# Row scaling folded into TensorE's turning of the token tiles, with a new loading and issue order at the start of a hybrid stream encoder

## The chip, the cores and the metric

The kernel runs on one core of one Trainium2 chip. The metric is the device time of that core in microseconds (us). A core has five engines with instruction streams of their own: TensorE (PE, matrix products, with its weight loads shown as PEld), VectorE (DVE), ScalarE (ACT), GpSimd (POOL) and SyncE (SP, which here only issues DMAs). They wait for each other through semaphores.

## The reference: one encoder step over 1024 + 64 tokens

The input is 1024 prompt rows and 64 sample rows of 2048 float32 numbers. Every row is first scaled to unit root mean square and by a vector, then multiplied by a wide matrix:

```python
def rmsnorm(x, g):
    r = lax.rsqrt(jnp.mean(xf * xf, axis=-1, keepdims=True) + EPS)
    return (xf * r * g.astype(jnp.float32)).astype(x.dtype)

h = rmsnorm(x, norm_g)
proj = jnp.einsum('btd,dc->btc', h, w_in)          # 2048 -> 10240 columns
xa, za, v, bg, cg, zb, ga, gb = jnp.split(proj, SPLIT_IDX, axis=-1)
ya = pool_mixer(xa) * silu(za)                     # trailing means over 2/4/8/16 frames, then a map
yb = bg * conv3(cg * v) * silu(zb)
merged = sigmoid(ga) * (ya @ w_proj_pool) + sigmoid(gb) * (yb @ w_proj_conv)
x = x + merged @ w_out
y = rmsnorm(x, final_norm_g)
```

Only the first `rmsnorm` and the first few products with `w_in` are touched by the change.

## The kernel before, in words

**Products.** All matrix products run in a rounded float32 type (f32r). To keep float32 accuracy each operand is held as a high part and a low part (what the high part leaves over), and each product is three terms: high weights by high tokens, high weights by low tokens, low weights by high tokens (`terms`, line 1323). One such product is 24 matmuls of 128 x 272. The big product is further divided by a recursive scheme that saves block products, so sums and differences of operand blocks are made on DVE. Weights come by DMA into three `raw` tiles, ACT makes the high part (`split_hi`, line 1573), DVE the low part (`split_lo`, line 1983), and DVE forms sums of weight blocks in three `sb` tiles (`weight_sum`).

**The opening.** The 1088 tokens are nine tiles `xn[0]` to `xn[8]` of 128 rows (the last has 64); in the listings of instructions they are called xn_104 to xn_112. Each tile goes through five steps:
1. two DMA queues (SP's and ACT's) load it, 1 MB a tile;
2. ACT squares it and sums each row (`square`, line 1870);
3. POOL makes `var` and `rstd`, one number a row (lines 1168 and 1171);
4. DVE or ACT multiplies the whole tile by `rstd` (`scale`, lines 2548 and 1877), in place;
5. TensorE turns it, 128 x 128 at a time (`turn`, line 1488): the tile's block is the stationary operand and the identity moves, in TensorE's transposing form. One turn (t, a) is eight such blocks, the half a of the columns of tile t, written to one of two PSUM tiles; `copy_turned` (lines 2560 and 2562, one on ACT at 1886) multiplies by `norm_g` on the way to SBUF.

There are 18 turns, two a tile. Their order stands in a table, `TURNS`, which PE and DVE both follow; turn i waits until turn i-2 has been copied out. Of the turns 11 stand ahead of the first product and the other seven between the first products. `turn_vectors` (lines 1494 and 1497) turns the small vectors and the state rows. Once the halves a = 0 of the tiles 0 to 4 are copied, `first_operand_hi(0)` (ACT, line 1648) and `first_operand_lo(0)` (DVE, line 2143) make the first token operand, and the first product can start. The first two weight groups use eight products each, from four operands f = 0 to 3; operand f = 2 needs the halves a = 0 of all nine tiles. From there on the kernel is a long list of products in a fixed order.

**Who sets the order.** No scheduler: each engine's instructions stand in the order of the code, and the waits are written by hand. The two queues and the lists of calls on ACT and DVE at the start are what the change rewrites.

Of the kernel before, what the change touches and what calls it, by code (L numbers as in the profile page):

```python
# [10 lines left out]
P = 128  # L11
# [4 lines left out]
def bass_hybrid_stream_step(nc, x_prompt, x_sample, state_pool, state_conv, norm_g, w_in, b_gate,  # L16
# [156 lines left out]
    for m in range(2 * NP):  # L173
        RAW_TILE[m] = (m if m < 3 else RAW_TILE[RAW_BEFORE[m]] if m in RAW_BEFORE else
                       RAW_Y if m == COUPLE_H1 else RAW_X)
        RAW_COUNT[m] = 1 + sum(RAW_TILE[k] == RAW_TILE[m] for k in range(m))
# [49 lines left out]
    with ExitStack() as ctx:  # L226
# [83 lines left out]
        sb = at("sb", SB0, [3, KQ * P])  # L310

# [140 lines left out]
        x_scaled_act = sem("x_scaled_act")  # L452
        x_scaled_dve = sem("x_scaled_dve")
# [120 lines left out]
        def prep_source(n):  # L574
# [10 lines left out]
            if q in (0, 5, 6):  # L585
# [262 lines left out]
        def _(sp):  # L848
# [294 lines left out]
        def _(pool):  # L1143
# [21 lines left out]
            for t in SQUARE_TURN:  # L1165
# [6 lines left out]
                    .then_inc(rstd_made, 1)  # L1172

# [136 lines left out]
        def _(pe):  # L1310
# [166 lines left out]
            def turn(i):  # L1477
# [50 lines left out]
            for i in range(11):  # L1528
                if i == 4:
# [3 lines left out]
            i = 11  # L1533
            for g in range(NC):
                for k, turns in enumerate((0, 0, 2, 4, 1, 0, 0, 0) if g == 0 else (0,) * 8):
# [25 lines left out]
        def _(act):  # L1561
# [298 lines left out]
            for t in (0, 1):  # L1860
                act.dma_start(xn[t][:, D // 2:D], x_rows(t)[:, D // 2:D]).then_inc(x_landed[t], 16)
# [824 lines left out]
```

## Time and profile before

| | |
|---|---|
| median of 3 runs | 2418.03 us (2417.90 to 2418.84) |
| the profiled execution | 2418.74 us |
| its span | 2416.9 us |
| PE busy | 99% of the span |
| DVE, ACT, POOL busy | 70%, 37%, 5% |
| mean granted TensorE clock | 0.997 of full |
| HBM read, written | 281.00 MB, 133.77 MB |

The profile is one execution. Times in it count from the start of the span. "Busy" of an engine excludes waiting and DMA issuing. A row of a timeline gives the start, the time from its first instruction's start to its last one's end, the line, the operation, the tile written and the tiles read, the count, and in brackets how long the engine had been idle and what released it. The duration of a single matmul record contains its latency, which neighbours overlap; what a matmul costs in a stream is read from the starts of two successive groups.

### The profile page before, as it was taken

To read this page: it belongs to the slowest core of one execution; us is meant where nothing else is said; L and a number is where in the kernel's file an instruction comes from. 1 tells how busy PE (TensorE), PEld (TensorE's weight loads), DVE (VectorE), ACT (ScalarE), POOL (GpSimd) and SP (SyncE) were. 2 spreads that over 40 slices of the span, in tenths; PEclk is the share of its full clock that TensorE was granted. 3 is DMA by queue.
4 is the path that set the end of the run, shared out by engine and by line. 5 is a ranking of instruction groups with operands and counts; after the bars stand their busy time and mean duration, and the time that the engine had idled before them with its cause. 6 is when DMAs were issued, how large, how long until landed. Compare 5 with 4: busy or idle time off the path is not lost.

```text
span 2416.9 us, 42656 instructions
## 1 busy us (share of the span) xinstructions
PE 2392.0 (99%) x17810; PEld 2331.3 (96%) x17810; DVE 1701.1 (70%) x2330; ACT 894.1 (37%) x1308; POOL 114.5 (5%) x218
## 2 busy tenths in 40 slices
PE   7999999999999999999999999999999999999998
PEld 7999999999999999999999999999999999888886
DVE  6676666666666686777868777765755887887676
ACT  6433333333333343323322222233533533532535
POOL 2010000000000000000000000000000011100000
PEclk9999999999999999999999999999999999999999
DMA  6663323232323454434433333245655768898656
GB/s 220 234 216 104 113 97 120 90 127 90 125 92 116 165 197 144 157 136 146 155 132 113 136 133 139 100 161 208 223 169 168 276 242 282 295 344 304 245 179 226
DMA packets 195695, 418.05 MB, mean 173 GB/s; under 512 B 12489, under 2 KB 113917, under 8 KB 180656
## 3 DMA queue, kind: packets, MB, share of 16 engines
q1 hardware_dynamic: 170672, 284.85, 35.1%
q0 software_dynamic: 23744, 125.24, 13.7%
q10 hardware_dynamic: 1088, 5.24, 0.6%
q8 instruction: 142, 2.33, 0.4%
q14 instruction: 49, 0.40, 0.1%
HBM read 281.00 MB, written 133.77 MB: 172 GB/s over the span
## 4 chain that ended last, share of the span: by engine, by line
PE 98%; DMA 1%; DVE 1%; issue 0%; ACT 0%; POOL 0%; ACTq 0%; DVEq 0%; POOLq 0%
PE ps L1323 76%; PE ps L1450 12%; PE ps L1365 7%; PE ps L1472 1%; PE ps L1512 1%; DMA xn<-in_x_prompt_dram 1%; PE ps L1488 0%; DVE ops L2143 0%; ACT ops L1648 0%; ACT junk L1870 0%; DVE out L2406 0%; DVE h0raw L2560 0%; DVE out L2459 0%; DVE xn L2548 0%; POOL rstd L1304 0%
## 5 line engine op out<-in xcount | busy, mean ns | idle before, releaser
L1323 PE MATMUL ps<-ops,hi 128*128 128x272 f32 x9760 | 1329.8, 288 | 0.2 <-DVE ops L2143 0.2
L1323 PEld LDWEIGHTS ps<-ops,hi 128*128 128x128 f32 x9760 | 1268.7, 188 | 0.7 <-DVE ops L2143 0.7
L1323 PE MATMUL ps<-ops,lo 128*128 128x272 f32 x4880 | 710.9, 288 | 0.0
L1323 PEld LDWEIGHTS ps<-ops,lo 128*128 128x128 f32 x4880 | 649.6, 188 | 0.0
L1573 ACT ACTIVATE hi<-sb 128x512 fp32r<-128x512 f32 x440 | 278.2, 632 | 579.0 <-PE ps L1323 444.2
L2123 DVE TENSOR_TENSOR pb<-pb,ps 128x544 f32<-128x544 f32 x330 | 237.4, 720 | 261.5 <-PE ps L1323 261.4
L1983 DVE TENSOR_TENSOR lo<-sb,hi 128x512 fp32r<-128x512 f32 x440 | 303.1, 689 | 151.4 <-ACT hi L1573 146.7
L1573 ACT ACTIVATE hi<-raw 128x512 fp32r<-128x512 f32 x264 | 166.7, 632 | 371.2 <-PE ps L1323 357.2
L1983 DVE TENSOR_TENSOR lo<-raw,hi 128x512 fp32r<-128x512 f32 x264 | 181.7, 689 | 104.4 <-ACT hi L1573 104.4
L1450 PE MATMUL ps<-ms_hi,mt 128*128 128x512 f32 x896 | 221.3, 389 | 0.0
L1450 PEld LDWEIGHTS ps<-ms_hi,mt 128*128 128x128 f32 x896 | 168.1, 188 | 34.9
L2041 DVE TENSOR_TENSOR pb<-pb,ps 128x544 f32<-128x544 f32 (+1 forms) x176 | 108.2, 614 | 69.7 <-PE ps L1323 66.2
L1590 ACT COPY pb<-ps 128x544 f32<-128x544 f32 (+1 forms) x160 | 83.6, 523 | 152.3 <-PE ps L1323 134.6
L2019 DVE TENSOR_TENSOR sb<-raw 128x512 f32<-128x512 f32 x183 | 125.3, 685 | 5.1 <-DMA raw<-in_w_in_dram 5.1
L1450 PE MATMUL ps<-ms_lo,mt 128*128 128x512 f32 x448 | 119.7, 389 | 0.0
L1619 ACT COPY pb<-ps 128x544 f32<-128x544 f32 x88 | 53.9, 612 | 157.1 <-PE ps L1323 141.2
L2406 DVE TENSOR_TENSOR out<-out,ps 128x512 f32<-128x512 f32 x100 | 68.1, 682 | 59.2 <-PE ps L1450 59.2
L1734 ACT CAST ms_hi<-ms 128x2048 fp32r<-128x2048 f32 x32 | 61.2, 1911 | 108.0 <-DVE ms L2354 73.4
L1450 PEld LDWEIGHTS ps<-ms_lo,mt 128*128 128x128 f32 x448 | 84.1, 188 | 17.5
L1365 PE MATMUL ps<-ops,hi 128*128 128x272 f32 x512 | 74.6, 288 | 0.0
L1740 ACT CAST mt<-mt_raw 128x2048 fp32r<-128x2048 f32 x28 | 53.5, 1910 | 54.0 <-DMA mt_raw<-opq 32.4
L2364 DVE TENSOR_TENSOR ms_lo<-ms,ms_hi 128x2048 fp32r<-128x2048 f32 x32 | 73.1, 2284 | 0.0
(164 smaller groups left out, 1564.6 us busy)
## 6 DMA issues: line engine op xcount, KB each, us to landing
raw<-in_w_in_dram SPq DMA_DIRECT2D x157, 512.0 KB, 3.9
pb<-part SPq DMA_DIRECT2D x39, 1088.0 KB, 6.8
part<-pb POOLq DMA_DIRECT2D x37, 1088.0 KB, 5.2
mt_raw<-opq SPq DMA_DIRECT2D x28, 1024.0 KB, 6.2
gates<-pb POOLq DMA_DIRECT2D x16, 1088.0 KB, 9.2
gate<-gates SPq DMA_DIRECT2D x32, 544.0 KB, 6.2
ms<-in_w_out_dram SPq DMA_DIRECT2D x16, 1024.0 KB, 9.9
ops_raw<-opq SPq DMA_DIRECT2D x15, 1088.0 KB, 7.3
```

What stands on the lines that cost most here:

```text
L1323: mm = nc.tensor.matmul(ps[b][:, c, 0:HC], w[:, w_slot, kt * P:(kt + 1) * P], operand[:, kt, half, c * HC:(c + 1) * HC], start=fresh and k ...
L1365: mm = nc.tensor.matmul(ps[b][:, c, 0:HC], w[:, s % R, k * P:(k + 1) * P], operand[:, kt, half, :], start=i in (0, 1, 5) and kt == 0 and w ...
L1450: mm = nc.tensor.matmul(dst, mt[n % 3][:, kt, half, t * P:(t + 1) * P], own[:, kt, :], start=fresh and kt == 0 and w is ms_hi and half == ...
L1573: nc.scalar.activation(split_of(hi, n), src, ACT.Copy).then_inc(w_hi, 1)
L1590: nc.scalar.copy(dst, src).then_inc(act_drained, 1)
L1734: nc.scalar.copy(ms_hi[(USES * p + e) % 3][:, :, :], src[:, :, :]).then_inc(ms_hi_made, 1)
L1983: nc.vector.tensor_tensor(split_of(lo, n), src, f32(split_of(hi, n)), ALU.subtract).then_inc(w_lo, 1)
L2019: nc.vector.tensor_tensor(sb_of(g, q), a, b, op).then_inc(s_made, 1)
L2041: each = nc.vector.tensor_tensor(own, own, src, ALU.add)
L2123: nc.vector.tensor_tensor(target(s), target(s), psum(s), ALU.add).then_inc(dve_drained, 1)
L2364: nc.vector.tensor_tensor(ms_lo[held][:, :, :], source_of(p, e)[:, :, :], f32(ms_hi[(USES * p + e) % 3][:, :, :]), ALU.subtract).then_inc( ...
L2406: nc.vector.tensor_tensor(own, own, m_tile(p, q, t), ALU.add).then_inc(m_added, 1)
```

## The change

The scaling of step 4 goes. Instead POOL multiplies the identity by `rstd` into a 128 x 128 tile `diag[t]`, and the turn multiplies by that in place of the identity. The turn is then no longer issued in the transposing form but as an ordinary float32 matmul: its result is the turned block with each token's column scaled. The nine diagonals lie where the `sb` tiles lie, so the first weight sum waits until all turns are done, and the fourth waits for `w_lo`.

All tiles are loaded in two column halves, the first half by SP and the second by ACT, in the order of the tiles; the first weight tile is loaded in two halves too, after tile 4 (`EARLY` is 5). ACT issues its halves of tiles 5 to 8 after its first two squares. The tables and the lists of calls are rewritten.

```diff
@@ at line 308 @@
+        diag = [at(f"diag{t}", SB0 + t * P * 4, [P]) for t in range(TT)]
@@ the order of the turns, of the squares @@
-        TURNS = ((0, 0), (0, 1), (1, 1), (1, 0), (3, 0), (2, 0), (4, 0), (2, 1), (3, 1),
-                 (5, 0), (5, 1), (7, 1), (7, 0), (8, 0), (8, 1), (6, 0), (4, 1), (6, 1))
+        TURNS = ((0, 1), (1, 1), (1, 0), (2, 0), (2, 1), (3, 0), (0, 0), (4, 0), (3, 1),
+                 (4, 1), (5, 0), (5, 1), (7, 0), (7, 1), (6, 0), (8, 0), (6, 1), (8, 1))
-        SQUARE_TURN = (0, 1, 3, 2, 4, 5, 7, 8, 6)
+        SQUARE_TURN = (0, 1, 2, 3, 4, 5, 7, 6, 8)
-        SCALED_ACT = (1, 5, 8, 6)
-        SCALED_DVE = (0, 3, 2, 4, 7)
-        COPIED_ACT = ((4, 1),)
+        COPIED_ACT = ((8, 1),)
@@ SP @@
-            for t in (0, 1):
-                sp.dma_start(xn[t][:, 0:D // 2], x_rows(t)[:, 0:D // 2]).then_inc(x_landed[t], 16)
-            for t in (3, 5):
-                sp.dma_start(xn[t][:, :], x_rows(t)).then_inc(x_landed[t], 16)
-            load_weights(0)
-            sp.dma_start(xn[7][:, :], x_rows(7)).then_inc(x_landed[7], 16)
+            for t in range(TT):
+                if t == EARLY:
+                    sp.dma_start(raw_pair(0)[:, 0:2, :], weights_of(0, 0)[:, 0:2, :]).then_inc(raw_landed[RAW_TILE[0]], 16)
+                sp.dma_start(xn[t][0:rows(t), 0:D // 2], x_rows(t)[:, 0:D // 2]).then_inc(x_landed[t], 16)
@@ POOL @@
+                pool.wait_ge(rstd_made, SQUARED_AT[t])
+                nc.gpsimd.tensor_scalar(diag[t][0:r, 0:r], ident[0:r, 0:r], rstd[0:r, t:t + 1], None, ALU.mult) \
+                    .then_inc(diag_made, 1)
@@ PE @@
-                if t in SCALED_ACT:
-                    pe.wait_ge(x_scaled_act, SCALED_ACT.index(t) + 1)
-                else:
-                    pe.wait_ge(x_scaled_dve, SCALED_DVE.index(t) + 1)
+                pe.wait_ge(diag_made, SQUARED_AT[t])
                 if i >= 2:
                     wait_copied(pe, i - 1)
                 for k in range(KE):
-                    mm = nc.tensor.transpose(flat[2 + i % 2][:, k * P:k * P + r],
-                                             xn[t][0:r, (a * KE + k) * P:(a * KE + k + 1) * P], ident[0:r, 0:r])
+                    mm = nc.tensor.matmul(flat[2 + i % 2][:, k * P:k * P + r],
+                                          xn[t][0:r, (a * KE + k) * P:(a * KE + k + 1) * P], diag[t][0:r, 0:r],
+                                          start=True, stop=True)
@@ PE, the turns ahead of and between the first products @@
-            for i in range(11):
-                if i == 4:
+            for i in range(12):
+                if i == 1:
                     turn_vectors()
-                for k, turns in enumerate((0, 0, 2, 4, 1, 0, 0, 0) if g == 0 else (0,) * 8):
+                for k, turns in enumerate((0, 2, 2, 1, 1, 0, 0, 0) if g == 0 else (0,) * 8):
@@ ACT @@
-            for t in (0, 1):
-                act.dma_start(xn[t][:, D // 2:D], x_rows(t)[:, D // 2:D]).then_inc(x_landed[t], 16)
-            for t in range(2, TT, 2):
-                act.dma_start(xn[t][0:rows(t), :], x_rows(t)).then_inc(x_landed[t], 16)
+            def load_second_half(t):
+                act.dma_start(xn[t][0:rows(t), D // 2:D], x_rows(t)[:, D // 2:D]).then_inc(x_landed[t], 16)
+
+            for t in range(EARLY):
+                load_second_half(t)
+            act.dma_start(raw_pair(0)[:, 2:4, :], weights_of(0, 0)[:, 2:4, :]).then_inc(raw_landed[RAW_TILE[0]], 16)
-            def scale(t):
-                r = rows(t)
-                own = xn[t][0:r, :]
-                act.wait_ge(rstd_made, SQUARED_AT[t])
-                nc.scalar.activation(own, own, ACT.Copy, scale=rstd[0:r, t:t + 1]).then_inc(x_scaled_act, 1)
@@ DVE @@
+                if SUM_COUNT[g, q] == 1:
+                    dve.wait_ge(x_turned, len(TURNS))
+                if SUM_COUNT[g, q] == 4:
+                    dve.wait_ge(w_lo, split_of_slot(NC * NQ + 1))
-            def scale(t):
-                r = rows(t)
-                own = xn[t][0:r, :]
-                dve.wait_ge(rstd_made, SQUARED_AT[t])
-                nc.vector.tensor_scalar(own, own, rstd[0:r, t:t + 1], None, ALU.mult).then_inc(x_scaled_dve, 1)
...
```

What it moves is seen in the engines' instruction lists. First PE, from the first turn on, before (xn_104 is tile 0, xn_105 tile 1; each pair of rows is one turn of eight blocks):

```order
L1488 MATMUL ps<-ident,xn_104 128x128 [waits x_scaled_dve]
L1488 MATMUL ps<-ident,xn_104 128x128 x7
L1488 MATMUL ps<-ident,xn_104 128x128 [waits x_scaled_dve]
L1488 MATMUL ps<-ident,xn_104 128x128 x7
L1488 MATMUL ps<-ident,xn_105 128x128 [waits h_copied_dve,x_scaled_act]
L1488 MATMUL ps<-ident,xn_105 128x128 x7
L1488 MATMUL ps<-ident,xn_105 128x128 [waits h_copied_dve,x_scaled_act]
L1488 MATMUL ps<-ident,xn_105 128x128 x7
L1494 MATMUL ps<-ident,vec_rows 128x64 [waits rows_landed]
L1497 MATMUL ps<-ident,state_rows 128x17 x8
```

and the same place now (diag_127 to diag_135 are the nine diagonals):

```order
L1484 MATMUL ps<-diag_127,xn_104 128x128 [waits diag_made]
L1484 MATMUL ps<-diag_127,xn_104 128x128 x7
L1491 MATMUL ps<-ident,vec_rows 128x64 [waits rows_landed]
L1494 MATMUL ps<-ident,state_rows 128x17 x8
L1484 MATMUL ps<-diag_128,xn_105 128x128 [waits diag_made]
L1484 MATMUL ps<-diag_128,xn_105 128x128 x7
L1484 MATMUL ps<-diag_128,xn_105 128x128 [waits h_copied_dve,diag_made]
L1484 MATMUL ps<-diag_128,xn_105 128x128 x7
L1484 MATMUL ps<-diag_129,xn_106 128x128 [waits h_copied_dve,diag_made]
L1484 MATMUL ps<-diag_129,xn_106 128x128 x7
```

The small turns of the vectors and the state, which wait for GpSimd's small loads, stand behind one turn now and stood behind four; tile 0's other half has gone to the seventh place.

Next PE behind the first product, before (its last term, the second product, and the turn of tile 7, which is xn_111):

```order
L1323 MATMUL ps<-ops,lo 128x272 [waits w_lo]
L1323 MATMUL ps<-ops,lo 128x272 x7
L1323 MATMUL ps<-ops,hi 128x272 [waits first_hi,w_hi,setup_copied]
L1323 MATMUL ps<-ops,hi 128x272 x7
L1323 MATMUL ps<-ops,hi 128x272 [waits first_lo]
L1323 MATMUL ps<-ops,hi 128x272 x7
L1323 MATMUL ps<-ops,lo 128x272 [waits w_lo]
L1323 MATMUL ps<-ops,lo 128x272 x7
L1488 MATMUL ps<-ident,xn_111 128x128 [waits h_copied_dve,x_scaled_dve]
L1488 MATMUL ps<-ident,xn_111 128x128 x7
```

and now:

```order
L1322 MATMUL ps<-ops,lo 128x272 [waits w_lo]
L1322 MATMUL ps<-ops,lo 128x272 x7
L1484 MATMUL ps<-diag_134,xn_111 128x128 [waits h_copied_dve,diag_made]
L1484 MATMUL ps<-diag_134,xn_111 128x128 x7
L1484 MATMUL ps<-diag_134,xn_111 128x128 [waits h_copied_dve,diag_made]
L1484 MATMUL ps<-diag_134,xn_111 128x128 x7
L1322 MATMUL ps<-ops,hi 128x272 [waits first_hi,w_hi,setup_copied]
L1322 MATMUL ps<-ops,hi 128x272 x7
L1322 MATMUL ps<-ops,hi 128x272 [waits first_lo]
L1322 MATMUL ps<-ops,hi 128x272 x7
```

Two turns now stand between the first and the second product; the six that are left after the first product come one or two at a time.

Last DVE's start, before:

```order
L2548 TENSOR_SCALAR xn_104<-xn_104,rstd 128x2048 [waits rstd_made]
L2567 COPY g_col<-ps 128x16 [waits g_turned]
L2560 TENSOR_TENSOR h0raw<-ps,g_col 128x8x128 [waits g_made,x_turned]
L2562 TENSOR_TENSOR h1raw<-ps,g_col 128x2x4x128 [waits g_made,x_turned] x2
L2560 TENSOR_TENSOR h0raw<-ps,g_col 128x8x128 [waits g_made,x_turned]
L2573 COPY state<-ps 128x136 [waits setup_turned]
L2548 TENSOR_SCALAR xn_107<-xn_107,rstd 128x2048 [waits rstd_made]
L2548 TENSOR_SCALAR xn_106<-xn_106,rstd 128x2048 [waits rstd_made]
L2560 TENSOR_TENSOR h0raw<-ps,g_col 128x8x128 [waits g_made,x_turned]
```

and now:

```order
L2557 COPY g_col<-ps 128x16 [waits g_turned]
L2559 COPY state<-ps 128x136 [waits setup_turned]
L2553 TENSOR_TENSOR h1raw<-ps,g_col 128x2x4x128 [waits g_made,x_turned] x2
L2564 COPY vec<-ps 128x64 [waits setup_turned]
L2551 TENSOR_TENSOR h0raw<-ps,g_col 128x8x128 [waits g_made,x_turned] x2
L2553 TENSOR_TENSOR h1raw<-ps,g_col 128x2x4x128 [waits g_made,x_turned]
L2551 TENSOR_TENSOR h0raw<-ps,g_col 128x8x128 [waits g_made,x_turned] x3
```

DVE has no scaling left, only copies; the copy of the state rows, which was behind four copies of turns, is ahead of all of them.

## Rows read from the trace of the kernel before

**Rows 1.** The page, engine totals: busy us, share of the span, instructions.

```profile
PE 2392.0 (99%) x17810; PEld 2331.3 (96%) x17810; DVE 1701.1 (70%) x2330; ACT 894.1 (37%) x1308; POOL 114.5 (5%) x218
```

**Rows 2.** Stretches: length, busy us by engine, clock, DMA share, GB/s.

```profile
8.19:30.86 22.67, 16.79 (x99) 14.61 (x99) 17.01 (x16) 17.84 (x16) 4.72 (x11) 0.85 1.03 360
30.86:50.75 19.89, 19.28 (x164) 18.58 (x162) 16.90 (x16) 15.33 (x14) 3.75 (x6) 1.00 0.19 59
50.75:87.00 36.25, 36.25 (x288) 36.25 (x289) 25.31 (x18) 18.01 (x26) 3.67 (x5) 1.00 0.51 184
```

**Rows 3.** The chain of waits, 0 to 75 us: start, us, what.

```profile
2.15 17.32 DMA xn<-in_x_prompt_dram
...
22.44 1.30 DVE xn L2548
...
37.58 1.75 PE ps L1488 x16
```

**Rows 4.** Timeline of ACT, the opening.

```profile
5.82 1.91 ACT L1870 ACTIVATE junk<-xn 128x2048 f32<-128x2048 f32 x1 [0.35 <-DMA xn<-in_x_prompt_dram]
...
8.91 1.91 ACT L1870 ACTIVATE junk<-xn 128x2048 f32<-128x2048 f32 x1 [1.09 <-DMA xn<-in_x_prompt_dram]
...
19.49 1.91 ACT L1870 ACTIVATE junk<-xn 128x2048 f32<-128x2048 f32 x1 [1.25 <-DMA xn<-in_x_prompt_dram]
...
27.05 2.01 ACT L1648 CAST ops<-h0raw 128x2176 fp32r<-128x2176 f32 x1 [0.51 <-DVE h0raw L2560]
```

**Rows 5.** Timeline of GpSimd (POOL), the opening.

```profile
1.18 0.29 POOL L1146 TENSOR_SCALAR_AFFINE_SELECT ident<-ident 128x128 f32<-128x128 f32 x1 [0.25 <-POOL ident L1144]
...
5.34 0.50 POOL L1163 DMA_DIRECT2D state_rows<-in_state_conv_dram  x1
7.91 0.18 POOL L1168 TENSOR_SCALAR var<-ssq 128x1 f32<-128x1 f32 x1 [2.07 <-ACT junk L1870]
8.18 0.56 POOL L1171 TENSOR_TENSOR rstd<-var,power 128x1 f32<-128x1 f32 x1
```

**Rows 6.** DMA issues, 0 to 75 us: count, KB each, us to landing.

```profile
state_rows<-in_state_conv_dram POOLq DMA_DIRECT2D x1, 8.0 KB, 9.4
```

**Rows 7.** Timeline of PE: turns and products.

```profile
10.12 6.15 PE L1488 MATMUL ps<-ident,xn 128*128 128x128 f32 x32 [1.67 <-DVE xn L2548]
16.20 0.27 PE L1494 MATMUL ps<-ident,vec_rows 64*128 64x64 f32 x1
16.40 0.66 PE L1497 MATMUL ps<-ident,state_rows 17*128 17x17 f32 x8
...
21.01 1.92 PE L1488 MATMUL ps<-ident,xn 128*128 128x128 f32 x8 [0.91 <-DVE xn L2548]
...
42.27 1.22 PE L1488 MATMUL ps<-ident,xn 64*128 64x64 f32 x16
...
73.99 2.18 PE L1323 MATMUL ps<-ops,hi 128*128 128x272 f32 x16
76.01 1.17 PE L1323 MATMUL ps<-ops,lo 128*128 128x272 f32 x8
77.01 2.18 PE L1323 MATMUL ps<-ops,hi 128*128 128x272 f32 x16
```

**Rows 8.** Timeline of PE, the last phase, 128x512 products.

```profile
2150.80 1.98 PE L1450 MATMUL ps<-ms_hi,mt 128*128 128x512 f32 x8
2152.61 1.07 PE L1450 MATMUL ps<-ms_lo,mt 128*128 128x512 f32 x4
2153.52 1.98 PE L1450 MATMUL ps<-ms_hi,mt 128*128 128x512 f32 x8
```

**Rows 9.** Timeline of DVE, the opening.

```profile
8.78 1.29 DVE L2548 TENSOR_SCALAR xn<-xn,rstd 128x2048 f32<-128x2048 f32 x1 [8.78 <-POOL rstd L1171]
...
12.12 1.23 DVE L2560 TENSOR_TENSOR h0raw<-ps,g_col 128x1024 f32<-128x1024 f32 x1 [1.98 <-PE ps L1488]
...
29.80 2.42 DVE L2143 TENSOR_TENSOR ops<-h0raw,ops 128x2176 fp32r<-128x2176 f32 x1
```

**Rows 10.** Stretches of two us, columns as in rows 2.

```profile
20.00:22.00 2.00, 1.09 (x6) 0.99 (x6) 2.00 (x2) 1.91 (x3) 0.33 (x2) 0.78 1.14 386
22.00:24.00 2.00, 1.15 (x6) 0.75 (x5) 1.65 (x3) 1.59 (x2) 0.64 (x3) 0.50 0.99 204
...
26.00:28.00 2.00, 2.00 (x11) 1.93 (x10) 1.52 (x2) 1.49 (x2) 0.00 (x0) 0.52 0.99 411
```

More of the change, by code:

```diff
@@ L175, in bass_hybrid_stream_step @@
                        RAW_Y if m == COUPLE_H1 else RAW_X)
-        RAW_COUNT[m] = 1 + sum(RAW_TILE[k] == RAW_TILE[m] for k in range(m))
+        RAW_COUNT[m] = 1 + sum(RAW_TILE[k] == RAW_TILE[m] for k in range(m)) + (RAW_TILE[m] == RAW_TILE[0])
     def operands_of(ph, o):
@@ L1891, in _ @@
             square(0)
+            load_second_half(5)
+            load_second_half(6)
             square(1)
-            scale(1)
+            load_second_half(7)
+            load_second_half(8)
+            square(2)
             square(3)
-            square(2)
             square(4)
             square(5)
-            scale(5)
+            split_hi(SLOT0)
             first_operand_hi(0)
-            split_hi(SLOT0)
             split_hi(SLOT0 + 1)
             square(7)
+            square(6)
+            split_hi(SLOT0 + 2)
+            square(8)
+            split_hi(SLOT0 + 3)
             first_operand_hi(1)
-            square(8)
-            split_hi(SLOT0 + 2)
-            square(6)
-            scale(8)
-            scale(6)
-            split_hi(SLOT0 + 3)
+            first_operand_hi(2)
             drain(SLOT0)
-            first_operand_hi(2)
             first_operand_hi(3)
             drain(SLOT0 + 1)
-            copy_turned(4)
+            split_hi(SLOT0 + 4)
+            copy_turned(8)
             drain(SLOT0 + 2)
-            split_hi(SLOT0 + 4)
             split_hi(SLOT0 + 5)
+            split_hi(SLOT0 + 6)
+            split_hi(SLOT0 + 7)
+            drain(SLOT0 + 3)
             first_operand_hi(4)
-            split_hi(SLOT0 + 6)
-            drain(SLOT0 + 3)
-            split_hi(SLOT0 + 7)
-            first_operand_hi(5)
             drain(SLOT0 + 4)
             drain(SLOT0 + 5)
+            first_operand_hi(5)
+            first_operand_hi(6)
             split_hi(NC * NQ)
-            first_operand_hi(6)
+            drain(SLOT0 + 6)
             split_hi(NC * NQ + 1)
+            first_operand_hi(7)
             split_hi(NC * NQ + 2)
-            drain(SLOT0 + 6)
-            first_operand_hi(7)
             for s in range(NC * NQ, NS):
@@ L2574, in _ @@
                 "p (j n) -> p j n", n=32)[:, :, 0:HALO]).then_inc(setup_copied, 1)
-            scale(3)
-            scale(2)
+            copy_turned(TURNS.index((0, 1)))
+            copy_turned(TURNS.index((1, 1)))
+            dve.wait_ge(setup_turned, 2)
+            nc.vector.tensor_copy(vec[:, :], flat[1][:, 0:NVEC]).then_inc(setup_copied, 1)
+            copy_turned(TURNS.index((1, 0)))
+            copy_turned(TURNS.index((2, 0)))
+            copy_turned(TURNS.index((2, 1)))
             copy_turned(TURNS.index((3, 0)))
-            scale(4)
@@ L2588, in _ @@
+            copy_turned(TURNS.index((7, 0)))
             split_lo(SLOT0 + 1)
-            scale(7)
-            copy_turned(TURNS.index((5, 1)))
+            copy_turned(TURNS.index((7, 1)))
+            split_lo(SLOT0 + 2)
+            split_lo(SLOT0 + 3)
             first_operand_lo(1)
-            split_lo(SLOT0 + 2)
-            copy_turned(TURNS.index((7, 1)))
-            copy_turned(TURNS.index((7, 0)))
+            copy_turned(TURNS.index((6, 0)))
             copy_turned(TURNS.index((8, 0)))
-            copy_turned(TURNS.index((8, 1)))
@@ L2608, in _ @@
+            weight_sum(NC * NQ + 1)
             split_lo(SLOT0 + 7)
-            first_operand_sum(2)
-            weight_sum(NC * NQ + 1)
+            first_operand_lo(5)
+            first_operand_lo(6)
+            first_operand_sum(3)
             split_lo(NC * NQ)
             weight_sum(NC * NQ + 2)
-            first_operand_lo(5)
             weight_sum(NC * NQ + 3)
             split_lo(NC * NQ + 1)
-            first_operand_sum(3)
-            first_operand_lo(6)
             split_lo(NC * NQ + 2)
```

28 lines of the change are left out of this document (10 added, 18 removed).

## The prediction

> **What bounds the kernel now.** I read the engine totals first, then the opening by stretches, then its chain of waits, then the timelines of the engines in the chain. TensorE is busy 2392.0 us [rows 1] of a span of 2416.9, so the time is the work on PE plus its idle time. From 50.75 us on PE does not stop: the stretch to 87 is full [rows 2], with products back to back. What comes later is not touched, so a shift of the point where PE becomes gapless passes to the end one for one. In the opening PE works 16.79 of the 22.67 us up to the first product at 30.86, and 19.28 of the next 19.89 [rows 2]. The chain shows what it waited for: the token tiles by DMA until 19.47, then square, `rstd`, the scaling at 22.44, turns, and the making of the operand [rows 3]. So there are two prices to compare: what the change saves of this idle time, and what it adds to PE's work.
>
> **What a turn costs.** Now: two turns, 16 blocks, take 1.75 us in the chain [rows 3], 0.87 us a turn or 109 ns a block; the sample tile's two turns take 1.22 us [rows 7]. The turn at 21.01 took 1.92 us for eight blocks [rows 7], at a granted clock that fell in that stretch to 0.50, which is 1.2 GHz of 2.4 [rows 10]. The first four took 6.15 us [rows 7].
>
> After: the identity becomes a diagonal with full float32 numbers and the transposing form goes. No row shows an ordinary float32 matmul, so I bound it. From below: a block costs what it costs now, 109 ns (a loss of speed below that has no reason, and a gain none either). From above: the kernel itself writes a float32 product as terms of high and low parts and leaves out the fourth; a complete one has four. Four streams each as dear as a block of today's turn give 436 ns, 3.5 us a turn. Between them, by the f32r products: 24 matmuls of 272 columns start 3.02 us apart (73.99 to 77.01) [rows 7], 126 ns each, and 12 of 512 columns start 2.72 us apart (2150.80 to 2153.52) [rows 8], 227 ns each. That is 0.42 ns a column and 12 ns fixed. Four terms of 128 columns are 227 ns as one stream of 512 columns, or 4 x (0.42 x 128 + 12) = 263 ns as four. I take 245 ns, 1.96 us a turn, since an ordinary product is nearer to these rows than to a turn. For the sample tile (64 columns, 256 in all, near a 272-column matmul) 138 ns, 1.1 us a turn.
>
> The Trainium skill, "FP8 and Floating Point Precision", section "TensorE Precision Notes", says that true FP32 makes four passes through the array. The same skill, "TensorE: Matmul & The Clock Gate", section "Terms", has the transposing form four times faster for FP32; by that a block would take four times 109 ns, which is my upper bound and a rival below. No run here shows either.
>
> **The start of PE's work.** The first square starts at 5.82 [rows 4] and `rstd` is there at 8.74 [rows 5]. Before, DVE's scaling (1.29 us, at 8.78 [rows 9]) followed, and the first turn began at 10.12 [rows 7]. Now POOL's diagonal follows. The nearest row of a 128x128 tile on POOL takes 0.29 us [rows 5], against 1.29 for a whole-tile operation on DVE; I take 0.45 with the hand-over: PE begins at about 9.3. Today's first blocks ran at the slow pace of the turn at 21.01 (the first four turns 1.54 us each against 0.87), so I give the first turn twice 1.96, to about 13.2. Next in PE's list stand the small turns of vectors and states. They wait for five small loads; the last is issued at 5.34 [rows 5] and lands 9.4 us later [rows 6], at about 14.75. Before, PE came to them at 16.20 [rows 7] and did not wait; now it waits some 1.5 us. They take 0.9 us (16.20 to 17.06 [rows 7]), so the second turn starts at about 15.7.
>
> **Is a turn ever late after that?** Tiles arrive every 2.7 us: between the squares at 8.91 and 19.49, both started by an arrival [rows 4], four tiles of 1 MB came, 2.65 us each. In the new order tile t lands at about 5.8, 8.8, 11.5, 14.2, 16.9; a square takes 2.1, `var`, `rstd` and the diagonal 1.3, so tile 4's diagonal is there at about 20.5. PE needs two turns a tile, 3.9 us, more than the 2.65 of an arrival. The turn (4, 0) is the seventh behind 15.7, so PE reaches it at 27.5. The loading in halves, the order of the squares and the removed scaling (five times 1.29 us on DVE, four times about 2 us on ACT) therefore end nothing that is waited for: I cost them at nothing, and what hides them is PE's own turning. The same holds for the copies, 1.23 us each on DVE [rows 9] against 1.96 a turn.
>
> **The first product.** Eleven turns behind 15.7 end at 15.7 + 11 x 1.96 = 37.3. The operand is not later: (4, 0) ends at 29.4, copied at 30.7, ACT's high part 2.0 [rows 4] to 32.7, DVE's low part 2.4 [rows 9] behind two copies to about 36. So 37.3 against 30.86: **+6.4 us**.
>
> **Behind it.** Before, five whole turns and the sample tile's two stood between the products: 5 x 0.87 + 1.22 = 5.6. Now four and two: 4 x 1.96 + 2 x 1.1 = 10.0. **+4.4 us**. What PE idled between 30.86 and 50.75: of 19.89 us [rows 2] the products before 50.75 are four whole ones (12.1) and a third of one (1.0), the turns 5.6, so 1.2 us, which the longer turns cover, because the operands f = 2 and 3 gain on PE: **-1.2 us**. The new waits of DVE for `x_turned` and `w_lo` stand ahead of weight sums that are needed only after the 16 products of the first two groups; nothing behind them is due earlier. Nothing.
>
> **Sum.** +6.4 + 4.4 - 1.2 = +9.6 us on the profiled execution's 2418.74, 2428.3. The median is 0.7 lower, so I forecast **2427.6 us**. As a function of a turn t in us the sum is 16.1 t - 22.0 (fifteen whole turns, and two of the sample's at 0.56 t): it crosses zero at t = 1.36, 170 ns a block. With 227 to 263 ns a block it is +7.3 to +11.9. If the small loads do not hold PE, 1.5 less. If the clock falls again, up to 3.5 more (seven us at half speed, as around 21 to 28 before, rows 10). The forecast's own range is 2423 to 2433.
>
> The clock is a place where the change could win. It stood at 0.50 to 0.53 between 22 and 28 us, and PE was turning at 26 to 28 without a break [rows 10]. The skill's "TensorE: Matmul & The Clock Gate", section "Part 4: PE-mode transpose", says that transposing work does not count as busy for the clock; this trace agrees, with 0.52 over two full us. By that rule ordinary matmuls would keep the full clock, which my sum assumes already; it saves no more.
>
> **Rival 1, the turn stays cheap.** If a float32 matmul with a diagonal streams like today's block (109 ns, 0.87 us a turn), PE is no longer the bound in the opening: the diagonal of tile 4 at 20.5, its turn to 21.4, copy to 22.7, high part to 24.7, low part behind two copies to about 27.7, while its first third runs ahead of that, so the products start in effect at 26.7 against 30.86 plus 0.4 of waiting, -4.6, and a little of the 1.2 behind: about -6 us, 2412. For it: only the form of the instruction differs, and a block is of the same size. Against it: the kernel pays three f32r terms and the splitting to avoid float32 products, which makes no sense at that price. It decides below 170 ns a block.
>
> **Rival 2, four times a turn's price.** 436 ns a block, 3.5 us a turn: 16.1 x 3.5 - 22.0 = +34, and the first slow turn then ends at 16.3 behind the small loads, +1.6: 2454. For it: today's block takes 109 ns, not the 66 ns that 128 columns of f32r would take, so something other than columns may set its pace, and that would be paid four times. Against: what makes the turn slow may belong to its form.
>
> **Rival 3, in between.** A block of 140 to 200 ns (two streams at 66 to 100) gives 1.1 to 1.6 us a turn, and the sum lies between -4 and +4 us: 2418, no change that can be told.
>
> **Chances.** Forecast (200 to 290 ns) 0.61; dearer, towards rival 2, 0.14; in between 0.13; rival 1 0.12. A measurement of this kernel tells about 0.2%, 4.8 us, from no change, so faster means below 2413.2 and slower above 2422.9. Rival 1 gives faster 0.11 with a rest in the same; the middle case gives most of same, 0.13; slower 0.76. The range reaches down to rival 1 and up past the forecast's own to where the dearer cases begin: 2413 to 2440, which leaves out half of rival 1 and about 0.08 above.
>
> **What would show it.** Right: groups of `ps<-diag,xn` with starts of eight blocks 1.8 to 2.1 us apart; PE without idle time from about 15.7; a wait of PE ahead of the small turns of about 1.5 us; the first product at 36 to 39 us; a gapless PE at the full clock from there; and the same work per product from 60 us to the end. Wrong: PE waiting for `diag` at tiles 2 to 5 (then the turn is cheap and arrival decides), a first product before 31 us, a granted clock of 0.5 in the turning, or a changed idle time of PE behind 60 us, for which I see no mechanism.

## The result and the profile after

| | before | changed |
|---|---|---|
| median | 2418.61 us (6 runs, 2417.90 to 2419.72) | 2426.45 us (6 runs, 2426.07 to 2428.91) |
| span of the profiled execution | 2416.9 us | 2424.1 us |

The ratio is 1.0034 with a 95% interval of 1.0021 to 1.0046: slower by 7.8 us. The forecast was 2427.6, slower.

The page of the changed kernel, engine totals, answers to [rows 1]:

```profile
PE 2404.5 (99%) x17954; PEld 2345.9 (97%) x17954; DVE 1695.9 (70%) x2325; ACT 886.4 (37%) x1304; POOL 119.7 (5%) x227
```

PE is busy 12.5 us longer in a span 7.2 us longer: it idles 5.3 us less and works 12.5 more. Its instruction count rose by 144, the number of blocks in 18 turns: each ordinary float32 block is recorded as two matmuls. The line of the turns says the same, with 288 records for these 144 blocks (kernel after; operation, count, duration min/median/max, first and last start):

```profile
L1484 PE MATMUL ps<-diag,xn x288: 272/275/582, 9.5 to 56.6; 128*128 128x128 f32 x128, 64*128 64x64 f32 x16
```

The timeline of PE in the changed kernel answers to [rows 7]; it holds nearly the whole story (start, us, what, count, and in brackets the idle time before):

```profile
9.51 3.56 PE L1484 MATMUL ps<-diag,xn 128*128 128x128 f32 x16 [0.99 <-POOL diag L1170]
13.00 0.27 PE L1491 MATMUL ps<-ident,vec_rows 64*128 64x64 f32 x1
13.20 0.66 PE L1494 MATMUL ps<-ident,state_rows 17*128 17x17 f32 x8
13.80 19.92 PE L1484 MATMUL ps<-diag,xn 128*128 128x128 f32 x176
33.47 2.24 PE L1322 MATMUL ps<-ops,hi 128*128 128x272 f32 x16
...
54.92 2.00 PE L1484 MATMUL ps<-diag,xn 64*128 64x64 f32 x16
...
59.97 2.18 PE L1322 MATMUL ps<-ops,hi 128*128 128x272 f32 x16
```

The 176 recorded matmuls from 13.80 on are eleven turns without a gap, up to the first product at 33.47: 1.79 us each, 112 ns a recorded matmul and 223 ns a block. After them PE waits for nothing longer than 0.2 us. A fixed place in the list is the sixth product, which starts at 59.97 now. In the kernel before it is this row:

```profile
52.85 2.18 PE L1323 MATMUL ps<-ops,hi 128*128 128x272 f32 x16
```

It is 7.1 us later now, which is the difference of the spans but for 0.1. From 100 to 400 us both are gapless at 100%.

What PE waited for from its first turn to its last instruction, before (us in total, times, longest; two waits of 0.2 us are left out, and the wait of 8.2 us for the row of `norm_g` at the very start, which the changed kernel has too, with 8.3):

```profile
PE ps L1488 <- DVE xn L2548: 5.4, 4, 1.9
PE ps L1488 <- DVE h0raw L2560: 0.4, 1, 0.4
```

and in the changed kernel, where only the wait for the first diagonal is left behind that:

```profile
PE ps L1484 <- POOL diag L1170: 1.0, 1, 1.0
```

### The profile page after: what moved, and what is told of

Its sections match the earlier page's. It is cut to its first block, busy times and chain, and to the rows that moved or that the text cites. A ratio compares the mean times of both kernels' runs of the same rounds, so it can differ in the third digit from the quotient of the medians.

```text
span 2424.1 us, 42950 instructions
## 1 busy us (share of the span) xinstructions
PE 2404.5 (99%) x17954; PEld 2345.9 (97%) x17954; DVE 1695.9 (70%) x2325; ACT 886.4 (37%) x1304; POOL 119.7 (5%) x227
## 4 chain that ended last, share of the span: by engine, by line
PE 99%; issue 0%; DVE 0%; DMA 0%; POOL 0%; ACT 0%; DVEq 0%; ACTq 0%; POOLq 0%
PE ps L1322 76%; PE ps L1449 12%; PE ps L1364 7%; PE ps L1484 1%; PE ps L1471 1%; PE ps L1509 1%; DMA xn<-in_x_prompt_dram 0%; DVE out L2403 0%; DVE out L2456 0%; DVEq L226 0%; POOL rstd L1303 0%; ACT squares L1766 0%; ACT squares L1775 0%; PE ps L1519 0%; DVE rest L2434 0%
```

## The experiments

Each was timed beside runs of the kernel before, and its ratio is to those. The times are medians. The medians of the kernel before in these groups lie between 2418.41 and 2419.26 us, so a difference of 1 or 2 us between two kernels of different groups says nothing.

**1. The form alone, undone.** In the changed kernel; the scaling by `rstd` is left out, so it computes without the first row norm:

```diff
-   mm = nc.tensor.matmul(dst, block, diag[t][0:r, 0:r], start=True, stop=True)
+   mm = nc.tensor.transpose(dst, block, ident[0:r, 0:r])
```

> The changed kernel with the transposing form and the identity again in the turns; the scaling by rstd is left out altogether, so it computes without the first row norm. All loads, orders and waits are those of the changed kernel (the turns still wait for the diagonals). Theory A (the form costs the time: two matmuls of 112 ns a block against one of 109): a turn takes 0.87 us, PE has idle time again before the first product, which starts near 27 to 28 us, and the median is about 2412, some 14 below the changed kernel. Rival B (the new order and loads cost it): the turns get cheap and the time stays within 3 us of 2426.

Measured: 2416.98 us (10 runs), ratio to before 0.9991 (0.9982 to 1.0001), 9.5 us below the changed kernel. So the form costs the time, and rival B falls: new order and loads are not what made it slower. But my 2412 was too low. PE in this kernel (the turns up to 27 us are of 128x128 blocks, eight a turn):

```profile
19.94 2.19 PE L1484 MATMUL ps<-ident,xn 128*128 128x128 f32 x16 [0.28 <-DVE h0raw L2550]
22.42 2.19 PE L1484 MATMUL ps<-ident,xn 128*128 128x128 f32 x16 [0.28 <-DVE h0raw L2550]
...
28.18 1.25 PE L1322 MATMUL ps<-ops,hi 128*128 128x272 f32 x8
...
33.12 1.96 PE L1484 MATMUL ps<-ident,xn 128*128 128x128 f32 x16 [1.25 <-POOL diag L1170]
```

With cheap turns DVE's copies set the pace: two turns every 2.48 us, 1.24 each, not 0.87. The first product came at 28.18, and the turns of tile 7 waited for its diagonal. The chain of waits says why that came late (start, us, what):

```profile
8.71 20.69 DMA xn<-in_x_prompt_dram
...
29.42 2.02 ACT junk L1868 x2
...
32.45 0.62 POOL diag L1170
```

The square started as soon as the tile was there, at 29.4: this wait is for the load. ACT, which issues the second halves of the tiles 7 and 8 only with its second square, issued them from 8.71 on. In the changed kernel the same square starts at 30.3 and PE does not wait for it. Of the PE work that the cheap form saves (about 17 us, an estimate: 16 turns at 1.79 less 0.87, and the sample tile's two at 1.9 less 0.6), 9.5 us reach the end. The rest is handed back as waiting, even without any scaling.

**2. The form alone, done.** In the kernel before:

```diff
-   mm = nc.tensor.transpose(dst, block, ident[0:r, 0:r])
+   mm = nc.tensor.matmul(dst, block, ident[0:r, 0:r], start=True, stop=True)
```

> The kernel before with one edit: the turns are ordinary float32 matmuls with the identity. The scaling, loads and orders of before stay, and the result is the same. Theory A: 16 turns rise from 0.87 to 1.79 us and the sample tile's two from 0.6 to 1.9, 17 us more PE work, of which 5 to 7 us fall into idle time of PE: about +10 to +12, 2428 to 2430. Rival B (new order costs it): within 2 us of 2418.6. Clock: if it fell at 21 to 28 us because transposing work does not count as busy, it is 1.00 there now; if it fell because PE had gaps, it falls here too unless the longer turns close the gaps.

Measured: 2431.89 us (4 runs), ratio 1.0050 (1.0034 to 1.0067), +13 us, a little above the 10 to 12 of theory A. So the form is dear in the old order too. By the medians it costs 5 us more there than the whole change does, which the other parts of the change would then give back; but the intervals of the two ratios overlap (1.0034 to 1.0067, and 1.0021 to 1.0046), so that gain is not shown. The trace is of the slowest of the four executions, 2435.24 us. The second question of the expectation was the clock (stretches of this kernel: length, busy us and counts of PE, PEld, DVE, ACT, POOL, then the granted clock, DMA share, GB/s):

```profile
20.00:22.00 2.00, 1.14 (x13) 0.85 (x11) 1.62 (x3) 1.91 (x3) 0.35 (x2) 1.00 1.13 367
22.00:24.00 2.00, 0.94 (x4) 0.95 (x5) 2.00 (x2) 1.58 (x2) 2.00 (x1) 0.74 0.91 189
24.00:26.00 2.00, 2.00 (x12) 2.00 (x11) 0.20 (x1) 0.82 (x1) 0.98 (x3) 0.50 1.08 314
```

It falls to 0.50 here too, at the end of a gap of 1.9 us, with ordinary matmuls. In experiment 1, with transposing work and only short gaps, it stays:

```profile
22.00:24.00 2.00, 1.65 (x14) 1.34 (x13) 1.88 (x3) 1.82 (x2) 0.00 (x0) 1.00 1.03 412
24.00:26.00 2.00, 1.67 (x14) 1.24 (x13) 1.89 (x3) 1.93 (x4) 1.37 (x3) 1.00 1.11 361
```

So the fall of the clock in [rows 10] needs no transposing work, and transposing work does not by itself bring it. The Trainium skill, "TensorE: Matmul & The Clock Gate", section "Part 4: PE-mode transpose", says that transposing work is not counted as busy in the same way; these two runs do not agree with it, and the measurement decides. That the gaps of PE bring the fall is only argued. The same execution of experiment 2 speaks against it: the clock fell a second time, to 0.50 from 54 to 60 us, where PE had no gap at all. The row (four turns, two of them the sample tile's):

```profile
50.91 10.77 PE L1488 MATMUL ps<-ident,xn 64*128 64x64 f32 x64
```

It lasts 10.5 us to the next product, where 7.4 are due at the full pace. These 3 us are about what sets this execution above the other three (2431.22 to 2432.45).

**3. The sample tile's diagonal 128 columns wide.**

```diff
-   ... diag[t][0:r, 0:r] ...
+   ... diag[t][0:r, :] ...
```

> The changed kernel with the sample tile's diagonal 128 columns wide (the upper 64 are zeros, and what they give is not read). Its two turns took 1.93 us each, more than the 1.79 of a whole tile, where I had forecast 1.1. Theory C (a stream of only 64 columns is slow in itself): with 128 columns a turn takes 1.79 or less. Rival D (the 64 rows or the weight load set the pace, the columns do not matter): it stays at 1.93. The whole time moves by 0.3 us at most and says nothing.

Measured: 2428.89 us, one execution. The sixteen recorded matmuls of one turn and the product behind them:

```profile
57.50 2.05 PE L1484 MATMUL ps<-diag,xn 64*128 64x128 f32 x16
59.48 2.28 PE L1322 MATMUL ps<-ops,hi 128*128 128x272 f32 x16
```

1.98 us to the next product, against 1.92 with 64 columns (54.92 to 56.84, the start of the product behind them). Theory C falls and rival D stands: twice the columns do not matter, and fewer do not help. The turn did not come down to the 1.79 us of a whole tile either: with 64 rows a recorded matmul takes 120 to 124 ns, against 112 with 128 rows. Why is open.

**4. Each block's diagonal in two matmuls of 64 columns.**

```diff
+   for n in range(0, r, 64):
+       mm = nc.tensor.matmul(dst[:, n:n + 64], block, diag[t][0:r, n:n + 64], start=True, stop=True)
```

> The changed kernel with each whole block's moving diagonal given in two matmuls of 64 columns, each with the block as stationary operand; the same result. One block of 128 columns takes 223 ns. Theory H (the columns set the pace): the pair takes about 223 to 260 ns, the time moves by less than 5 us. Rival I (the two weight loads of an ordinary float32 matmul set it, as the sample tile's 240 ns at 64 and at 128 columns suggests): each half takes about 220 to 240, a pair 440 to 480, a turn 3.6 to 3.8 us, and the time rises by about 28 us, to 2455.

Measured: 2495.37 us, one execution, +69 against the changed kernel. PE in the first product's high terms and between later products:

```profile
93.24 3.97 PE L1322 MATMUL ps<-ops,hi 128*128 128x272 f32 x16
...
108.71 5.61 PE L1485 MATMUL ps<-diag,xn 128*128 128x64 f32 x48
...
117.35 3.68 PE L1485 MATMUL ps<-diag,xn 128*128 128x64 f32 x32
```

32 matmuls of 64 columns in 3.5 us (117.35 to the next product at 120.84) are 109 ns each: the same as with 128 columns. Rival I's reading holds: a float32 block costs two recorded matmuls of about 110 ns, whatever its columns up to 128, and a pair of halves costs four. No run tells the weight load from a fixed price of the matmul. The forecast of 2455 was 40 us low, because before 93 us each such matmul took about 215 ns; even the first product's high terms took 3.97 us instead of 2.25. PE was at the half pace for more than 80 us, from its first turn at 9.86 on, without a gap.

**5. The same with PE started early**, by 24 ordinary blocks of 128 columns:

```diff
+   for k in range(24):
+       nc.tensor.matmul(flat[2][:, 0:P], ident[:, :], ident[:, :], start=True, stop=True)
```

> The kernel with each whole block turned in two matmuls of 64 columns, now with the 24 ordinary 128-column blocks of the identity on PE ahead, from 1.5 us. Without them it ran at the half pace (215 ns a recorded matmul) until its first 272-column products at 93 us, and at 115 ns after them. Theory K (the half pace is a state that wide streams end and narrow ones keep): here the turns start at the full pace, 112 to 116 ns a recorded matmul, 3.6 us a turn, and stay there or fall back some us later; if they stay, the time is about 2426 + 16 x 1.8 = 2455, if they fall back about 2490. Rival (64 columns cost 215 ns whatever the state until products come between): 2494.

Measured: 2495.50 us, one execution. The stretches of PE (length, busy, granted clock, DMA share, GB/s):

```profile
5.00:9.00 4.00, 3.82 (x34) 1.00 1.03 408
9.00:14.00 5.00, 4.33 (x28) 0.76 1.03 369
14.00:20.00 6.00, 6.00 (x33) 0.50 1.04 395
20.00:40.00 20.00, 20.00 (x96) 0.50 0.62 189
...
60.00:90.00 30.00, 30.00 (x143) 0.50 0.19 75
```

34 matmuls in 3.82 us of the early work are the full pace, 112 ns each. Then the narrow ones run, and the clock falls to 0.50 (1.2 GHz) some 2 us into them and stays there for 75 us of gapless PE. Of theory K's two outcomes falling back is what happened (about 2490 forecast); that narrow streams keep the state they find fell. It is not the whole rule: behind the first product the same narrow matmuls kept the full pace for 7 us (64 of them at 110 ns, in both experiments), and then in this execution the clock fell again near 111 us, with no gap of PE, and the third product ran at the half pace. Note the clock column: in experiment 4 the same pace stood beside 1.00 all along. The column seems to read 1.00 until the first recorded change (in experiment 4 the trace holds no record of the clock before about 98 us, where the pace doubles), so at the start of an execution the pace of the matmuls tells the clock, not the column.

**6. The changed kernel started early**, with the same 24 blocks.

> The changed kernel with 24 ordinary float32 blocks of the identity by the identity on PE from 1.5 us on, into a PSUM tile that the first turns overwrite; nothing else. The first turn took 3.56 us against 1.79 for the later ones, and in other executions the slow pace lasted until 16 or 18 us. Theory F (PE is slow after standing still): the first turn takes 1.79 us, the second follows at once unless the small loads hold the vectors' turns until 12.3, and 1 to 2 us go: 2424.5 to 2425.5, with less scatter. Rival G (the slow start comes from the loads that fill the DMA engines then, or anything else at that time): the first turn stays at 3.5 us, the time at 2426.5.

Measured: 2425.97 us (6 runs, 2425.42 to 2426.06), 0.5 below the changed kernel, beside different runs of before (ratio 1.0029, 1.0017 to 1.0040). PE:

```profile
9.51 2.05 PE L1484 MATMUL ps<-diag,xn 128*128 128x128 f32 x16 [0.28 <-POOL diag L1170]
12.28 0.27 PE L1491 MATMUL ps<-ident,vec_rows 64*128 64x64 f32 x1 [0.71 <-DMA state_rows<-in_state_conv_dram]
```

Theory F holds in the trace: the first turn is at the full pace, so the slow start of PE is its standing still, not the loads. Of the 1.5 us that it gains half ends in a wait for the small loads (0.71 us), and the first product starts 0.7 us earlier, at 32.74. The scatter is smaller. The gain of 1 to 2 us that theory F gave did not come; 0.5 us is too small to call shown.

**7. The old loads in the changed kernel.** In words: instead of first halves on SP and second halves on ACT, in the order of the tiles, with the first weight tile in halves after tile 4, the tiles 0 and 1 come in halves, then 3, 5, the first weight tile and 7 whole on SP, and 2, 4, 6 and 8 whole on ACT. For SP (excerpt):

```diff
-            for t in range(TT):
-                if t == EARLY:
...
+            for t in (0, 1):
+                sp.dma_start(xn[t][:, 0:D // 2], x_rows(t)[:, 0:D // 2]).then_inc(x_landed[t], 16)
+            for t in (3, 5):
+                sp.dma_start(xn[t][:, :], x_rows(t)).then_inc(x_landed[t], 16)
+            load_weights(0)
```

> The changed kernel with the loads of before: tiles 2 and on whole, 3, 5, 7 on SP and 2, 4, 6, 8 on ACT, all issued at the start, the first weight tile whole. The order of squares and turns stays. My prediction's step: loads hidden behind PE's turning are worth nothing against the changed kernel, 2426.5. Rival E: tile 2 lands at about 16.2 instead of 12.3, its diagonal comes at 19.7, and PE, which reaches its turn at 17.5, waits 2 us: 2428.5, with tile 4's later landing hidden (diagonal 23, PE there at 26).

Measured: 2429.87 us (4 runs, 2427.34 to 2430.93), ratio to before 1.0041 (1.0026 to 1.0056): 3.4 above the changed kernel by the medians, but with its lowest run inside the other's range and the intervals of the ratios overlapping, so that the old loads are slower is likely and not shown. PE:

```profile
9.47 3.60 PE L1486 MATMUL ps<-diag,xn 128*128 128x128 f32 x16 [1.23 <-POOL diag L1172]
14.64 0.27 PE L1493 MATMUL ps<-ident,vec_rows 64*128 64x64 f32 x1 [1.56 <-DMA state_rows<-in_state_conv_dram]
```

Neither theory had the right place. Tile 2's square started at 14.70 and its diagonal was not waited for: rival E's mechanism did not occur. PE waited 1.56 us for the small loads, which with the new loads are there by 12.3 (experiment 6). The issues of that last small load say the same (count, KB, us to landing), in the changed kernel and in experiment 6:

```profile
state_rows<-in_state_conv_dram POOLq DMA_DIRECT2D x1, 8.0 KB, 7.1
state_rows<-in_state_conv_dram POOLq DMA_DIRECT2D x1, 8.0 KB, 6.9
```

against 9.4 us before [rows 6]. That is the wait that I had forecast for the changed kernel. Behind it PE ran slow again for some us, with a granted clock of 0.50 from 17 to 19. In this execution the first product started at 36.74, 3.3 us later than in the changed kernel: the wait is half of that, the slow stretch behind it the other half.

**8. New loads, old form.** The turns transpose, tiles 0 to 4 and 7 are scaled on DVE, 5, 6 and 8 on ACT; the order of tiles and loads is that of the changed kernel, with nine turns ahead of the first product. Against the kernel before (excerpt):

```diff
-   SCALED_ACT = (1, 5, 8, 6);  SCALED_DVE = (0, 3, 2, 4, 7);  SQUARE_TURN = (0, 1, 3, 2, 4, 5, 7, 8, 6)
+   SCALED_ACT = (5, 6, 8);  SCALED_DVE = (0, 1, 2, 3, 4, 7);  SQUARE_TURN = (0, 1, 2, 3, 4, 5, 7, 6, 8)
```

> The new loading order with the form of before: tiles loaded in halves in their order, turns transposing with the identity, tiles 0 to 4 and 7 scaled on DVE and 5, 6, 8 on ACT, nine turns ahead of the first product and 2, 2, 3, 2 between the next ones. Same result. Theory A (only the form costs; the loads are a gain of their own): tile 4's first turn ends near 22.7 us against 25.8 before, the first product starts near 26.5, but DVE's copies and ACT's squares then pace the rest: PE gapless from 48, some 2 us less than before, 2416 to 2417. Rival B: no better than before, 2418.9, because ACT and DVE have the same work in the same stretch.

Measured: 2419.45 us (11 runs), ratio 1.0004 (0.9995 to 1.0013): no difference from before, as rival B had it. Its PE:

```profile
10.17 3.67 PE L1486 MATMUL ps<-ident,xn 128*128 128x128 f32 x16 [1.77 <-DVE xn L2555]
...
20.59 1.09 PE L1486 MATMUL ps<-ident,xn 128*128 128x128 f32 x8 [1.38 <-DVE xn L2555]
22.92 2.29 PE L1486 MATMUL ps<-ident,xn 128*128 128x128 f32 x16 [1.24 <-DVE xn L2555]
...
27.46 1.23 PE L1321 MATMUL ps<-ops,hi 128*128 128x272 f32 x8 [0.97 <-ACT ops L1646]
29.82 1.27 PE L1321 MATMUL ps<-ops,hi 128*128 128x272 f32 x8 [1.14 <-DVE ops L2150]
...
52.50 2.18 PE L1321 MATMUL ps<-ops,hi 128*128 128x272 f32 x16
```

The first product starts 3.4 us earlier than before, but the sixth at 52.50 against 52.85. Of the 3.1 us lost in between, 1.7 are the two turns that stand behind the first product here and stood ahead of it before. Some 1.1 are waits of PE: 1.14 for the low part of the first operand and 0.54 for a copy, against 0.17 and 0.37 before. Rival B's reason, that ACT and DVE have the same work in the same stretch, fits (ACT works from 23.7 to 43.7 with two gaps of 1 us), but no row shows PE waiting for the operand f = 2, which needs all nine tiles.

The rows bear on the clock too. All of PE's work up to 27.46 is transposing here, and its pace rose under it: two turns took 3.67 us at 10.17 and 2.29 at 22.92. The gaps of 1.38 and 1.24 us at 20.59 and 22.92 are longer than those around the slow turn of the kernel before (0.91 and 0.85 us, behind one of 1.95), and the pace stayed full.

**9. The same, started early** with the 24 blocks of experiment 5.

> The kernel with the new loading and the transposing turns (previous one) with the same 24 ordinary blocks on PE from 1.5 us on. Theory F: its first turns run at the full pace and end a few us earlier, but PE is ahead of the tiles and of DVE there, so little of it reaches the end: 0 to 1 us less than without. If the clock falls behind the gaps nevertheless, nothing.

Measured: 2418.69 us (11 runs), ratio 1.0000 (0.9992 to 1.0009): level with before and with the previous one within the intervals. In the profiled execution nothing was gained at all. The first two turns run at the full pace (1.97 us), but then:

```profile
14.32 2.20 PE L1486 MATMUL ps<-ident,xn 128*128 128x128 f32 x16 [2.21 <-DVE h0raw L2569]
...
20.54 1.97 PE L1486 MATMUL ps<-ident,xn 128*128 128x128 f32 x8 [1.38 <-DVE xn L2557]
...
28.29 1.23 PE L1321 MATMUL ps<-ops,hi 128*128 128x272 f32 x8 [0.52 <-ACT ops L1648]
```

The clock fell at about 21 us, to 0.50, behind the same gap of 1.38 us as in experiment 8, where it did not, and the first product started 0.8 us later than there. What differs ahead of it is the early start and, since the first turns are done sooner, a longer standing still at 12.1 to 14.3. So what makes the clock fall in the opening stays open: transposing or ordinary work does not decide it, and neither does the gap just before.

**10. Diagonals for tiles 0 to 4 only.**

```diff
+   if t < EARLY:  mm = nc.tensor.matmul(dst, block, diag[t][0:r, 0:r], start=True, stop=True)
+   else:          mm = nc.tensor.transpose(dst, block, ident[0:r, 0:r])   # scaled before on DVE (5, 7) and ACT (6, 8)
```

> The changed kernel with the diagonals for tiles 0 to 4 only. The turns of tiles 5 to 8 are transposing again, on tiles that are scaled before: 5 and 7 on DVE, 6 and 8 on ACT, where they stand between the other work. Same result. Theory A, additive: six whole turns get 0.92 us cheaper and the sample's two 1.3, 8.1 us less PE work, 2418.4, as fast as the kernel before. Rival L (with the turns cheap, the scaling on ACT and DVE is waited for again, as in the kernel before): PE idles 1 to 3 us before the later products, 2419.5 to 2421.5.

Measured: 2425.18 us (10 runs, 2423.01 to 2425.93), ratio to before 1.0023 (1.0014 to 1.0032). It is only 1.3 below the changed kernel by the medians, 2.7 by the two ratios, where the additive price said 8.1. Three of its runs lie at 2423.0 to 2423.3 and seven at 2425.0 to 2425.9; the trace is of one of the three. What PE waited for:

```profile
PE ps L1499 <- DVE xn L2566: 2.5, 2, 1.8
PE ps L1327 <- DVE ops L2161: 1.3, 2, 1.1
```

Rival L's mechanism, and more of it than I gave: 3.8 us of new waits in the trace, for the scaling and the operand behind it, where 1 to 3 were forecast. PE's dear turns had hidden a chain on ACT and DVE that is nearly as long. The waits leave 4.3 of the 8.1 us, and the span is 2.8 shorter; the rest, and the slower seven runs, are not explained.

## Why the prediction was right, step by step

**The direction and the mechanism.** The ordinary form is dearer than what its idle time hides, PE is gapless from the second turn on, and nothing behind 60 us changes. Experiments 1 and 2 show the form as the cause, from both sides: -9.5 us undone, +13 done alone.

**The price of a block.** Forecast 245 ns between 109 and 436; measured 223 ns, a turn 1.79 instead of 1.96. The size was close and its reason was wrong, so the closeness is luck. I had priced columns, four terms of 128. The records show two matmuls of 112 ns a block, and experiments 3 and 4 that columns up to 128 do not enter. The same mistake mis-sized the sample tile: forecast 1.1 us a turn for its 64 columns, measured 1.92, which is not less than a whole tile. Rival 2's four times today's block did not come: two times did. Of the Trainium skill's two rules that were weighed, the four passes ("FP8 and Floating Point Precision", section "TensorE Precision Notes") are not what the records show as matmuls, two a block, and no run tells what one record holds; and the factor of four for the transposing form ("TensorE: Matmul & The Clock Gate", section "Terms") is 223 against 109 here, two.

**The first product, +6.4 forecast, +2.6 measured** (33.47 against 30.86). Two terms failed, both too dear. The wait of 1.5 us for the small loads did not come: I took their landing time from the trace of before (9.4 us), but it depends on the big loads beside them: with the new ones the last small load takes 7.1 us and has landed by 12.5, before PE is there at 13.0. Experiment 7 has the wait back with the old loads. The other is the turn, 11 x 0.17 = 1.9 us. The first turn at the slow pace was right: 3.56 us against 3.9.

**Behind it, +4.4 forecast for the turns, +5.4 measured.** Four turns and two of the sample's took 11.0 us in the chain of waits:

```profile
36.72 3.57 PE ps L1484 x32
...
43.29 3.71 PE ps L1484 x32
...
50.20 1.78 PE ps L1484 x16
...
54.98 1.93 PE ps L1484 x16
```

That is one more than the 10.0 forecast: the sample tile's two turns cost 1.65 more and the four whole ones 0.7 less. From the first to the sixth product PE takes 4.5 us longer than before, so the turns cover 0.9 of idle time, where 1.2 was forecast.

**The sum**: 2.6 + 5.4 - 0.9 = 7.1 us in the traces and 7.8 in the medians, against 9.6 forecast. Errors of both signs met; with the sample tile priced right and the rest as it was, I would have been at +11.

**What was costed at nothing.** The copies, squares and removed scalings: right in the changed kernel, but only because PE's turning hid them; experiments 1 and 10 show how little is behind that cover. The loads were probably not worth nothing: with the old ones the changed kernel's median is 3.4 us higher, of which the trace shows 1.56 as the wait for the small loads, but the intervals overlap (experiment 7).

**Rival 1** had its mechanism right and its price wrong: with turns at today's price the kernel is at 2416.98, not 2412. I let PE follow the arrival of tiles and overlooked that DVE's copies (1.23 us) are then longer than a turn (0.87), and that tile 7 lands only at 29.4 (experiment 1).

**The clock.** "This trace agrees" was wrong, and the rows of before could have said so. One stretch with transposing work at 0.52 was consistent with the rule, but the first four turns, 6.15 us [rows 7], are transposing work too, and they went from the slow pace to the full one: at the slow pace four would have taken more than 7 us (two took 3.67 in experiment 8). Experiments 1, 2 and 8 confirm that the form does not decide; what does is open. In the changed kernel's profiled execution the clock did not fall.

## What to carry to other kernels

Folding a row scale into a transposition by a diagonal is not free in float32: it doubles the matmuls, here for 0.92 us more a tile half, to save a scaling of 1.29 us on an engine that was not the bound. Before pricing an instruction form that the trace lacks, ask how many instructions of the engine it becomes, and whether its time grows with its size at all; before taking a landing time from a trace, ask what stood in front of it in the queues. When the busiest engine gets more work, what it covers looks free; the same items are not free once that work goes again.

## What the runs showed of the hardware

- An ordinary float32 matmul of a 128x128 block by 128 columns is recorded as two matmuls, 223 ns together; the transposing form as one, 109 ns. With 64 columns each of the two still takes about 110 ns (32 in 3.49 us, experiment 4). For a block of 64 rows it is 120 ns with 64 columns (changed kernel) and 124 with 128 (experiment 3).
- Ordinary float32 work without a gap does not always hold TensorE's clock. With blocks of 128 and 64 rows it fell to 0.50 from 54 to 60 us in one execution (experiment 2). With 64-column matmuls, after 128-column blocks at the full pace it fell to 0.50 and stayed there for 75 us, and fell once more near 111 us (experiment 5); behind the first product the same work kept the full pace for 7 us. From standing still, such work did not raise the pace in more than 80 us (experiment 4). One execution each.
- Half pace at the start of PE's work is seen in the starts of the matmuls (218 ns apart instead of 112, the first turn of the changed kernel) while the clock column reads 1.00. In the executions profiled, experiment 4 and the three with work ahead aside, it ended between 13 and 18 us, which moves the first product by up to 2.5 us (33.47 in the changed kernel, 36.00 in experiment 3). PE work ahead of the turns removed it (experiment 6).
- The clock rose under transposing work alone. The pace stayed full behind a gap of 1.38 us in one execution (experiment 8) and the clock fell to 0.50 behind the same gap in another (experiment 9).
- A load of 8 KB issued by GpSimd at 5.34 us landed 9.2 to 9.4 us later with the old loads (before, experiments 2 and 7) and 6.9 to 7.3 with the new (the changed kernel and the other experiments).
